# A quarter of the weighted sums of expert rows, moved from TensorE to VectorE

## The reference

```python
def block(tb):
    q = (tb @ w_pq).reshape(PEER_BLOCK, PEER_HEADS, 2, PEER_HALF)
    s = jnp.einsum('thcd,ckd->thck', q, sub_keys).astype(jnp.float32)
    s_top, i_top = lax.top_k(s, PEER_TOPK)
    ...
    best_s, pos = lax.top_k(cand_s, PEER_TOPK)
    idx = jnp.take_along_axis(cand_i, pos, axis=-1)
    gate = jax.nn.softmax(best_s, axis=-1).astype(tb.dtype)
    act = jax.nn.gelu(jnp.einsum('thkd,td->thk', peer_u[idx], tb), approximate=False)
    return jnp.einsum('thk,thkd->td', gate * act, peer_v[idx])
```

## Time and profile before

| | |
|---|---|
| time, median of 3 runs | 5646.52 us (5639.93 to 5648.68) |
| time of the profiled execution | 5650.95 us |
| its span | 5649.2 us |
| mean granted clock of PE | 0.944 |
| PE matmul busy | 4764.8 us (84%) |
| DVE busy | 2784.6 us (49%) |
| ACT busy | 1154.4 us (20%) |
| POOL busy | 1447.5 us (26%) |
| gathers (queue of POOL) | 1140.92 MB |
| other transfers of SP's queue | 229.89 MB |

### The profile page before, as it was taken

The page is one execution under the profiler, slowest core; times in us unless marked ns, Lnnn a source line. Parts: engine busy times, 40 slices in busy tenths (PEclk is TensorE's granted clock), DMA queues, the critical chain, the costliest instruction groups (busy, mean ns, idle before and its releaser), DMA issues.

```text
span 5649.2 us, 54093 instructions
## 1 busy us (share of the span) xinstructions
PE 4764.8 (84%) x19467; PEld 3031.7 (54%) x19467; DVE 2784.6 (49%) x6843; ACT 1154.4 (20%) x2943; POOL 1447.5 (26%) x1188
## 2 busy tenths in 40 slices
PE   5999999997878478489997799987799977899876
PEld 3777777775656357246563355643365633545431
DVE  2344444442555301674447654457744376544564
ACT  1233222222232201111211112111112111111111
POOL 0111111110111100243334433334433243333343
PEclk8999999997989799799999999999999999999999
DMA  1000000000111232599999998999999899999998
GB/s 66 24 27 27 23 24 27 27 13 35 47 39 39 95 125 88 223 406 374 352 347 405 408 392 353 371 371 392 410 372 355 339 416 390 373 403 401 400 411 361
DMA packets 233941, 1377.55 MB, mean 244 GB/s; under 512 B 34016, under 2 KB 49120, under 8 KB 89632
## 3 DMA queue, kind: packets, MB, share of 16 engines
q0 software_dynamic: 156672, 1140.92, 50.3%
q1 hardware_dynamic: 75856, 229.89, 11.0%
q10 hardware_dynamic: 1232, 4.46, 0.2%
HBM read 1349.77 MB, written 25.40 MB: 243 GB/s over the span
## 4 chain that ended last, share of the span: by engine, by line
PE 33%; DMA 19%; DVE 8%; POOL 2%; issue 1%; ACT 1%; SPq 0%; POOLq 0%; DVEq 0%; ACTq 0%
DMA back_rows<-in_peer_uv,back_picked_index 17%; PE psum_bank L1733 16%; PE psum_bank L1749 13%; DVE back_rows L2020 4%; POOL back_rows L1705 2%; DMA back_weights<-in_w_heads_ssm 1%; PE psum_bank L1867 1%; ACT back_diagonal L1895 1%; PE psum_bank L1777 1%; PE psum_bank L1764 1%; DMA back_weights<-in_w_pq 1%; DVE back_position L2152 1%; DVE back_sums L2153 1%; DVE back_position L2159 0%; DVE back_sums L2250 0%
## 5 line engine op out<-in xcount | busy, mean ns | idle before, releaser
L1733 PE MATMUL psum_bank<-back_rows,back_diagonal 128*128 128x512 f32 (+1 forms) x4352 | 2025.5, 613 | 373.8 <-ACT back_diagonal L1895 373.7
L2020 DVE SCALAR_TENSOR_TENSOR back_rows<-back_rows,back_tokens 128x1024 f32<-128x1024 f32 x1088 | 1321.9, 1223 | 1172.1 <-DMA back_rows<-in_peer_uv,back_picked_index 1166.6
L1705 POOL DMA_INDIRECT back_rows<-in_peer_uv,back_picked_index x1088 | 1219.1, 1120 | 2434.3 <-PE psum_bank L1733 1865.0
L1733 PEld LDWEIGHTS psum_bank<-back_rows,back_diagonal 128*128 128x128 f32 (+1 forms) x4352 | 806.8, 192 | 1467.2 <-issue 872.2
L1887 ACT ACTIVATE back_gelu<-back_dots 128x2 f32<-128x2 f32 x544 | 110.3, 203 | 2230.4 <-DVE back_rows L2020 2230.3
L445 PE MATMUL psum_bank<-x_normed,dn_weights 128*128 128x384 f32 (+1 forms) x1536 | 529.0, 488 | 12.7 <-DMA dn_conv_w<-in_dn_conv_w 12.7
L753 POOL TENSOR_TENSOR dn_block<-dn_lower,dn_level_masks 128x1152 f32<-128x1152 f32 x56 | 146.8, 2628 | 1005.1 <-DVE dn_lower L831 892.5
L445 PEld LDWEIGHTS psum_bank<-x_normed,dn_weights 128*128 128x128 f32 x1536 | 287.8, 198 | 153.9 <-issue 22.7
L1895 ACT ACTIVATE back_diagonal<-const_ident,back_gelu 128x128 f32<-128x128 f32 x1024 | 347.2, 386 | 0.1
L1749 PE MATMUL psum_bank<-back_normed,back_weights 128*128 128x256 f32 (+1 forms) x1280 | 272.2, 370 | 25.5 <-DVE back_normed L2073 20.7
L1749 PE MATMUL psum_bank<-back_heads_or_q,back_weights 128*128 128x256 f32 (+1 forms) x1280 | 262.9, 364 | 33.4 <-DMA back_weights<-in_w_heads_dn 21.2
(11 more groups left out here) (365 smaller groups left out, 4813.6 us busy)
## 6 DMA issues: line engine op xcount, KB each, us to landing
back_weights<-in_w_pq SPq DMA_DIRECT2D x80, 512.0 KB, 7.6
back_weights<-in_w_heads_dn SPq DMA_DIRECT2D x40, 512.0 KB, 6.9
back_weights<-in_w_heads_ssm SPq DMA_DIRECT2D x40, 512.0 KB, 5.9
back_weights<-in_w_xq SPq DMA_DIRECT2D x40, 512.0 KB, 6.8
back_weights<-in_w_xo SPq DMA_DIRECT2D x40, 512.0 KB, 7.9
back_rows<-in_peer_uv,back_picked_index POOLq DMA_INDIRECT x1088, 11.3
dn_weights<-in_w_dn SPq DMA_DIRECT2D x8, 2048.0 KB, 7.4
ssd_w_xz<-in_w_xz SPq DMA_DIRECT2D x8, 1024.0 KB, 4.7
```

The costliest lines, as they stand in the source:

```text
L1705: nc.gpsimd.indirect_dma_start(out=uv[:, m % RING, :], out_offset=None, in_=d["peer_uv"], in_offset=bass.IndirectOffsetOnAxis(ap=index[:, ...
L1733: mm = nc.tensor.matmul(ACC[half_][0:t, :], diag[:, m % TURNED, 0:t], uv[:, m % RING, D_MODEL + 512 * half_:D_MODEL + 512 * half_ + 512], ...
L2020: op = nc.vector.scalar_tensor_tensor(uv[:, m % RING, 0:D_MODEL], uv[:, m % RING, 0:D_MODEL], 1.0, x[:, i % 2, :], ALU.mult, ALU.mult, acc ...
```

## The change

Of every four slots the fourth (`SHARE = 4`) no longer goes to ACT and PE. DVE multiplies its v row by the weight and adds it to a partial sum in SBUF, `part` (the first one of a tile only multiplies). The pass stands behind the gate multiply of the group, in every second group, and waits for it. It signals `part_used`, for which POOL waits beside `used`. At a tile's end PE adds `part` to `ACC` by a multiplication by the identity (for the last tile, by the folded one). `part` takes the place of the buffer y in SBUF: y is now written into the tile's tokens' buffer `x`, which must be stored before it is filled with the tokens of the tile after the next. The mean square is taken in two halves that are written over `ACC`, so that `acc_taken` is signalled behind them.

```diff
+    SHARE = 4
+    added = lambda m: m // SHARE
+    weighed = lambda m: m - m // SHARE
...
-        y, norm = sb("y", [P, D_MODEL]), sb("norm", [P, 1])
+        ssq, norm = sb("y_squares", [P, 2]), sb("norm", [P, 1])
+        part = sb("partial_sum", [P, D_MODEL])
...
                         if m >= RING and k % PAIR == 0:
-                            pool.wait_ge(used.sem, used.at(m + PAIR - RING))
+                            pool.wait_ge(used.sem, weighed(m + PAIR - RING))
+                        if m >= RING and k % PAIR == 0 and added(m + PAIR - RING):
+                            pool.wait_ge(part_used.sem, added(m + PAIR - RING))
...
                         m = SLOTS * i + k
+                        if m % SHARE == SHARE - 1:
+                            continue
                         for half_ in range(2):
-                            mm = nc.tensor.matmul(ACC[half_][0:t, :], diag[:, m % TURNED, 0:t],
+                            mm = nc.tensor.matmul(ACC[half_][0:t, :], diag[:, weighed(m) % TURNED, 0:t],
...
+                    if n - 1 == ENDS[i]:
+                        pe.wait_ge(part_used.sem, added(SLOTS * i + slots_of(i)))
+                        for half_ in range(2):
+                            mm = nc.tensor.matmul(ACC[half_][0:t, :], const["ident"][:, :] if i < LAST else fold[:, :],
+                                                  part[:, 512 * half_:512 * half_ + 512], start=False, stop=True)
+                        mm.then_inc(part_taken.sem, 1)
...
                         nc.vector.tensor_tensor(gel[:, i % 2, a:a + PAIR], gel[:, i % 2, a:a + PAIR], gate[:, i % 2, a:a + PAIR],
                                                 ALU.mult).then_inc(weight_ready.sem, 1)
+                        m = SLOTS * i + a + PAIR - 1
+                        if m % SHARE == SHARE - 1:
+                            first = a + PAIR == SHARE
+                            if first and i:
+                                v.wait_ge(part_taken.sem, part_taken.at(i))
+                            v.wait_ge(weight_ready.sem, weight_ready.at(n))
+                            scale, src = gel[:, i % 2, a + PAIR - 1:a + PAIR], uv[:, m % RING, D_MODEL:2 * D_MODEL]
+                            if first:
+                                op = nc.vector.tensor_scalar(part[:, :], src, scale, None, ALU.mult)
+                            else:
+                                v.wait_ge(part_used.sem, added(m))
+                                op = nc.vector.scalar_tensor_tensor(part[:, :], src, scale, part[:, :], ALU.mult, ALU.add)
+                            op.then_inc(part_used.sem, 1)
...
-                    v.wait_ge(used.sem, used.at(SLOTS * i + slots_of(i)))
+                    v.wait_ge(part_taken.sem, part_taken.at(i + 1))
                     for half_ in range(2):
-                        op = nc.vector.tensor_copy(y[0:t, 512 * half_:512 * half_ + 512], ACC[half_][0:t, :])
+                        op = nc.vector.tensor_copy(x[0:t, i % 2, 512 * half_:512 * half_ + 512], ACC[half_][0:t, :])
+                    settle(op)
+                    v.wait_ge(vec.sem, vec.now())
+                    for half_ in range(2):
+                        own = x[0:t, i % 2, 512 * half_:512 * half_ + 512]
+                        op = nc.vector.scalar_tensor_tensor(ACC[half_][0:t, :], own, 1.0, own, ALU.mult, ALU.mult, accum_out=ssq[0:t, half_:half_ + 1])
                     op.then_inc(acc_taken.sem, 1)
...
                 def take_tokens(i):
                     v.wait_ge(tokens_turned.sem, tokens_turned.at(i + 1))
+                    if i > 1:
+                        v.wait_ge(y_stored.sem, y_stored.at(i - 1))
```

More of the change, by code:

```diff
@@ L1890, in step @@
                         act.wait_ge(weight_ready.sem, weight_ready.at(n))
-                        if PAIR * n > TURNED:
-                            act.wait_ge(used.sem, used.at(PAIR * n - TURNED))
+                        m = SLOTS * i + PAIR * g + PAIR
+                        if weighed(m) > TURNED:
+                            act.wait_ge(used.sem, weighed(m) - TURNED)
                         t = rows_of(i)
                         for k in range(PAIR * g, PAIR * g + PAIR):
-                            op = nc.scalar.activation(diag[:, (SLOTS * i + k) % TURNED, 0:t], const["ident"][:, :] if i < LAST else fold[:, :],
+                            m = SLOTS * i + k
+                            if m % SHARE == SHARE - 1:
+                                continue
+                            op = nc.scalar.activation(diag[:, weighed(m) % TURNED, 0:t], const["ident"][:, :] if i < LAST else fold[:, :],
                                                       ACT.Copy, scale=gel[:, i % 2, k:k + 1])
@@ L1912, in store @@
                     act.wait_ge(y_ready.sem, y_ready.at(i + 1))
[L1913 removed]
+                    act.dma_start(y_out[P * i:P * i + rows_of(i), :], x[0:rows_of(i), i % 2, :]).then_inc(y_stored.sem, 16)
                 beside = Beside(step, ENDS, AFTER)
```

14 lines of the change are left out of this document (6 added, 8 removed).

## The result

| | before | changed |
|---|---|---|
| median | 5647.6 us (5639.93 to 5648.91, 4 runs) | 5579.83 us (5575.78 to 5586.31, 4 runs) |
| profiled execution, its span | 5650.95, 5649.2 us | 5580.52, 5578.7 us |
| mean granted clock | 0.944 | 0.897 |

The ratio is 0.9884, with a 95% interval of 0.9869 to 0.99: faster by 1.2%. The forecast was 5577.0, within 5515 to 5650.

The account below looks back on a forecast made before the run. PE was taken to bound the dense stretches, gathers the rankings. Long stretches -90, fourth -5, rankings +20, tile ends +5 gave -70: 5581 us profiled, 5577 median, range 5515 to 5650.

Parts of the forecast that it names:

- Long stretches: Three dense stretches beside projections, PE the bound: 30 us won in each, 90 in all, bounds 8 and 45 each.
- OUT: Attention-input projection in a long stretch: 13.78 us per output falls to 12.9, full streams packing imperfectly; 7 us won.
- XQ and XO: Query and output projections in a long stretch: 6.88 us per output falls to 6.4; 8 us won.
- PQ: PEER query projection in a long stretch: PE still bounds it; 9.5 of the 10.3 us won.
- other 24 groups: Groups beside norms and attention in a long stretch: 5.5 us won of a possible 20.6.
- Fourth stretch: Dense stretch for the samples, weight loads and DMA share of 0.96 in its chain: 5 us won, 0 to 29.
- Rankings: Tokens' top-16 searches, eight: DVE's passes at 1.31 us make it late, ring absorbs 5.2 us; 2.5 lost each, 20 in all.
- Tile ends: Four tiles ending beside projections: DVE's squares delay `acc_taken` about 1.4 us; 5 us lost, 0 to 11; very end 0.
- The clock: Longer PE gaps put more rankings partly at 1.2 GHz: counted 0; as a rival 46 us, 5623, chance 0.08.
- DMA is full already: OUT, XQ and XO give nothing, 15 us per long stretch are left: about 5622 us; chance 0.18.
- Weight loads take PE's place: In OUT PE waits for weights if landing takes about 12 us or more; at 13.5, some 5676 us; chance 0.14.
- PE's whole share is won: Long stretches win 135 us, the fourth 29, rankings cost nothing: about 5485 us; chance 0.08.

Follow-up runs that it names:

- experiment 3: Changed kernel, but every fourth sum, except one per tile, is left out on both PE and DVE: 5541.19 us, ratio 0.9813.
- experiment 10: Every second sum off PE in dense stretches only, with DVE doing one pass per tile and the others left out: 5506.69 us, ratio 0.9757.
- experiments 1 to 3: Changed kernel with the share in dense stretches only, 5564.26 us; beside rankings, at start and end only, 5672.17 us; on neither engine, 5541.19 us.
- experiments 5 and 6: Changed kernel with DVE's share only in the first halves of the rankings, 5657.14 us; only in the second halves, 5663.51 us.
- experiments 8 and 9: Accumulators released earlier at tile ends: in the changed kernel, 5583.69 us; in the kernel of experiment 4, 5517.21 us.
- experiment 7: Changed kernel, but DVE takes only one weighted sum of each tile, nine in all, and PE all others: 5653.1 us, ratio 1.0013.
- experiment 4: Changed kernel, but DVE takes every second weighted sum in dense stretches and none in rankings: 5512.65 us, ratio 0.9768.

## Why the prediction was right, point by point

**Long stretches: -90 forecast, -89.4 measured.** The mechanism is the forecast one, PE's work where PE was the bound. That the sum is right to 1 us is luck: its terms are wrong and cancel. OUT was to give 7 us and gave 10.9; XQ and XO together 8, and gave 15.4; PQ 9.5, and gave 8.4. The "other 24 groups" were to give 5.5 and cost 5: the norms +8.7, the attention -2.1, the index sums -1.6. Two steps failed. One is "two streams at a full share seldom pack perfectly": in OUT and XO they do, 412 and 417 GB/s at 1.01, and PE comes down to its own need, 12.06 us for most outputs of OUT. The other is that the 24 groups beside norms and attention would win anything: the bytes that are moved in a stretch stay the same, and what the sections do not wait for any more is waited for in the norms behind them, where PE idles at 420 GB/s. A limit on the average of a stretch does not show in the section in which one looks for it. In the first norm about 2 of the 4.4 us belong not to the transfers but to the pass that stands in its chain, by experiment 3.

**Fourth stretch: -5 forecast (0 to -29), -2.4 measured.** The reason given, a DMA share of 0.96, was not tested by itself. It fits: even with half of the sums off PE the stretch gave only 10, and with DVE's passes gone too (experiment 10) 11.5, with the share at 0.99 from 4725 to 5115 us.

**Rankings: +20 forecast, +22.2 measured.** The mechanism is the forecast one: experiments 1 to 3 put the loss on DVE's passes, experiments 5 and 6 most of it on those in the part where DVE is full anyway. The price of a pass was right. The rest of the term was not, and that it comes out at 20 is in part luck. The ring took up less than was counted on: DMA below 1.0 in the heavy steps, which the forecast named as a sign of being wrong, is there, 0.89 to 0.97. That DVE's pass "releases no later than PE does" was wrong for the 36 waits shown above. And the loss is not 2.5 us in each of eight, but about 4 in the five rankings with 34 groups and, up to the index sums, 2.4 in the three with 26 (157.7 to 159.6 us before, 160.8 to 161.2 now). Of these 2.4 the latter get back 1.7 behind the index sums, where the next tile's gathers wait for the ranking's indices and PE works on two groups without a pause (14.0 us before, 12.3 now). The kernel before shows that place at the end of its second ranking, with PE busy throughout, no gather issued by POOL and DMA at half its rate:

```profile
3097.00:3107.00 10.00, 10.00 (x60) 7.37 (x59) 5.82 (x14) 1.62 (x8) 0.00 (x0) 1.00 0.52 216
```

That the ring takes up some lateness agrees with the 30 us for which DMA keeps its 1.01, but is not shown; a longer ring, which would test it directly, was not tried.

**Tile ends: +5 forecast (0 to 11), the end itself 0; together +7 measured (2 to 12).** The reason given for the 5 found no support: taking the wait for `acc_taken` away won nothing that could be measured (experiments 8 and 9). What makes up the 7 is open but for the end. The "0" at the very end was wrong. From the start of the last weighted sums to the end it was 16.4 us before, and is 19.5 now (18.4 in the kernel of experiment 7, where PE does four matmuls more than before). PE's timeline there in the changed kernel, which answers to the earlier trace rows:

```profile
5559.19 8.26 PE L1742 MATMUL psum_bank<-back_rows,back_diagonal 128*64 128x512 f32 x12 [3.26 <-ACT back_diagonal L1914]
5567.29 1.88 PE L1749 MATMUL psum_bank<-back_partial_sum,back_folded_ident 128*64 128x512 f32 x4
```

Sixteen records as forecast, but the first twelve take 8.26 us where sixteen took 7.08: after an idle gap of 3.26 us the granted clock is 0.64 in these twelve, where it was 1.00 before.

**The clock: counted as 0, rightly for the rankings.** It fell from 0.94 to 0.84 in the third, and experiment 3 shows 0.88 at no cost worth reading. The Trainium skill, "TensorE: Matmul & The Clock Gate", section "HAM oscillation — how this bites in real kernels", says that waits between PE's pieces of work drop it to half its clock. This trace agrees: behind the gap of 3.26 us PE's weight loads follow each other every 0.86 us until 5564.4, at the 1.2 GHz level, and every 0.43 from 5565.1 on. That the lower clock costs time is not so where the transfers set the pace, by experiment 3. It is so at the last twelve matmuls, where no transfer runs beside them.

**Rivals.** *DMA is full already* is half right: before the change it was not quite full in OUT and XO (0.97 to 0.99), and it is full there and in the norms after it; the second quarter of the sums (experiment 4) gave a third of the first, nearly all of it in PQ and XQ. *Weight loads take PE's place* came near. The median landings of the attention-input weights grew, those of one half to just below the 12 us from which the rival decides; SP's issues in the changed kernel (KB each, median us to landing; before, 6.9 and 5.9):

```profile
back_weights<-in_w_heads_dn SPq DMA_DIRECT2D x40, 512.0 KB, 11.0
back_weights<-in_w_heads_ssm SPq DMA_DIRECT2D x40, 512.0 KB, 7.8
```

PE waited for them a little, 13.9 us in seven waits for the second kind over the whole part, against 10.4 in four before. *PE's whole share is won* fails for the transfers, at which even half of the sums off PE ends (experiments 4 and 10).

## What to carry to other kernels

Give work to a second engine stage by stage, not everywhere: the same passes that were free over a stretch where PE was the bound (experiment 3 against the changed kernel) cost about 4 us in a ranking where DVE was full, and taking them out there while doubling their number elsewhere was worth as much again as the whole change. When a stage is relieved, count the bytes of the whole stretch against the transfer rate first, as a floor (382 us by that count in experiment 4, 395 to 397 measured); sections that become faster can hand the wait on to the next one. A wait that appears in the profile is worth nothing until something shows that it has no cover: 7.5 us of one were removed here for no gain that could be measured.

## What the runs showed of the hardware that was not expected

Gathers and weight loads through two queues together reached 410 to 420 GB/s at a share of 1.01 (OUT and XO of the changed kernel and of experiment 4), practically what gathers alone reach beside a ranking (420); I had counted on losing some 3% to their mixing (12.9 us in place of 12.48 for an output of OUT).

The issue of a gather on POOL took 0.93 to 0.96 us for most and 2.42 to 2.52 for some in the heavy part of a ranking. The Trainium skill, "SBUF — State Buffer", section "🔬 SBUF: two separate sides", describes how some DVE operations shut GpSimd out of a port that both use, so that it cannot write the descriptors of a transfer that it issues. No run here shows such an effect of DVE's passes on the mean issue: it was 1120 ns before and 1153 in the changed kernel, but 1162 in the kernel without passes. POOL's group in the changed kernel and in that of experiment 3 (count, busy us, mean ns):

```profile
L1712 POOL DMA_INDIRECT back_rows<-in_peer_uv,back_picked_index x1088 | 1254.6, 1153 | 2326.8 <-PE psum_bank L1742 1529.9
```

```profile
L1715 POOL DMA_INDIRECT back_rows<-in_peer_uv,back_picked_index x1088 | 1263.9, 1162 | 2286.7 <-PE psum_bank L1745 1666.0
```
